# The dummy products that TensorE runs in the waits of the delta-rule core and of the attention and RWKV core are taken out

## The chip, the cores and the metric

The kernel runs on one core of one Trainium2 chip. The metric is device time in microseconds; the median of three runs stands for a kernel. The core has five engines that run at the same time, each through its own list of instructions in order: TensorE (PE: products of matrices; its weight loads are shown apart as PEld), VectorE (DVE), ScalarE (ACT), GpSimd (POOL) and SyncE (SP, which issues the transfers here). Engines wait for one another by semaphores. TensorE's clock has two levels, 1.2 and 2.4 GHz; the profile tells which was granted when, as a share of full speed.

## What is computed

Two transformer blocks on one sequence of 256 tokens, width 1024, float32. The first is two layers of gated feed-forward networks around a mixer: a short convolution in layer 0, a gated delta rule in layer 1. The second block mixes sparse attention (8 heads of 64, in three branches) with an RWKV-7 recurrence (8 heads of 64) and ends in a convolutional feed-forward network.

The two recurrences are computed in chunks of 64 tokens. The delta rule, for 16 value heads with a 128 x 128 state each:

```python
a = jnp.where(strict, jnp.einsum("bhncd,bhnsd->bhncs", k_beta, k) * decay, 0.0)
t_inv = lax.linalg.triangular_solve(eye + a, jnp.broadcast_to(eye, a.shape), left_side=True, lower=True)
...
v_new = u_n - jnp.einsum("bhcd,bhde->bhce", w_n, state)
o = jnp.einsum("bhcd,bhde->bhce", q_g_n, state) + jnp.einsum("bhcs,bhse->bhce", qk_n, v_new)
state = state * jnp.exp(gl_n)[..., None, None] + jnp.einsum("bhcd,bhce->bhde", k_tail_n, v_new)
```

RWKV-7, whose reference is a step per token:

```python
sa = jnp.einsum('bhvk,bhk->bhv', state, a_t)
state = state * w_t[:, :, None, :] + sa[..., None] * b_t[:, :, None, :] + v_t[..., None] * k_t[:, :, None, :]
y = jnp.einsum('bhvk,bhk->bhv', state, r_t)
```

## The kernel before

Most of the time goes into products with weights. SP streams them in tiles of 256 KB, ScalarE and VectorE split each into a high and a low part (L389, L399), and TensorE multiplies high by high, low by high and high by low (L425 to L427). In two stages no weights are streamed, and TensorE works on small products between other engines' steps:

- The delta rule. `GatedDelta.core_pe` runs for four blocks B of four value heads, one behind the other. A block computes keys by keys and keys by queries (L1535, L1536), sums of log decays (L1541, L1546), inverts eight triangular 64 x 64 pairs (`Inverse.pe`), joins the halves (L1484, L1490), and then goes through the chunk: values (L1557), state (L1563), state by keys and queries (L1570, L1571), and outputs (L1576, L1579, L1583). VectorE, ScalarE and GpSimd turn one product's result into the next one's operand.
- The mixer of the second block. `nsa_pe` runs attention for eight units u: scores of unit u + 1 (`scores_pe`, L2200, L2201), then, when VectorE has made the matrix P of unit u, its transposes (L2164, L2166) and the values of unit u - 1 (`values_pe`, L2188). After it the RWKV core's `core_pe` runs for two blocks Bt of four heads: 32 products of decayed keys and queries (L2384 to L2387), the same `Inverse.pe`, two sets of products (L2397, L2405), and four steps c. In each step but the first TensorE multiplies the state M (L2422, L2423), waits for VectorE's N1, multiplies it by the inverse (L2430), waits for SA, and multiplies again (L2438); after every second step come the outputs (L2448, L2449).

`Inverse.pe` transposes, multiplies and waits for five levels: per level two transposes of each half (L950), then 8 products of 64 x 64 by 32 columns (L958), and 16 products (L965) behind VectorE's masked copy. It begins with 16 products in `start_pe` (L944).

TensorE follows its list in order. Between a group of products and the wait that follows it, this list has calls of `keep_clock` (L481), which multiplies the identity by a matrix of ones (128 x 128 each, float32) a given number of times into a PSUM bank that holds nothing of use at that moment; nobody reads the result and no semaphore is tied to it. There are 25 such products in each delta-rule block (4 in the inversion, 5 before it, 7, 3 and 6 after it), 8 in each attention unit, and 35 in each RWKV block (4 in the inversion, 4 before the steps, and three times 3 in each of the steps 1 to 3): 234 in all, each of which is two records of the trace, as all float32 products here are.

Of the kernel before, what the change touches and what calls it, by code (L numbers as in the profile page):

```python
# [19 lines left out]
P = 128  # L20
# [167 lines left out]
def build(nc, ins, out, stages):  # L188
# [28 lines left out]
    with ctx:  # L217
# [262 lines left out]

        def keep_clock(pe, count, bank=aux[1]):  # L481

            for _ in range(count):
                nc.tensor.matmul(bank[:, 0:P], ident[:, :], ones[:, :], start=True, stop=True)  # L484
# [416 lines left out]
        class Inverse:  # L901
# [107 lines left out]
            def pe(self, pe, r):  # L1009

                hs = range(len(self.parts))
                for h in hs:
                    self.start_pe(pe, r, h)
                keep_clock(pe, 4)
                for l in range(1, self.levels):
                    for h in hs:
                        self.x_pe(pe, r, l, h)
                    for h in hs:
                        self.u_pe(pe, r, l, h)
# [16 lines left out]
        class GatedDelta:  # L1036
# [478 lines left out]
            def core_pe(self, pe, B):  # L1515
# [32 lines left out]
                keep_clock(pe, 5)  # L1548
# [10 lines left out]
                keep_clock(pe, 7, acc[0][0])  # L1559
# [6 lines left out]
                keep_clock(pe, 3, acc[0][0])  # L1566
# [6 lines left out]
                keep_clock(pe, 6, acc[0][0])  # L1573
# [113 lines left out]
        class Mixer:  # L1687
# [436 lines left out]
            def nsa_pe(self, pe):  # L2124
# [28 lines left out]
                for u in range(8):  # L2153
# [3 lines left out]
                    keep_clock(pe, 8, acc[0][0])  # L2157
# [213 lines left out]
            def core_pe(self, pe, Bt):  # L2371
# [36 lines left out]
                keep_clock(pe, 4, acc[0][1])  # L2408
                for c in range(4):
# [3 lines left out]
                    if c:  # L2413
                        keep_clock(pe, 3, tr[1])
                        pe.wait_ge(DV.sem, DV.at["M", Bt, c - 1])
                        pe.wait_ge(AC.sem, AC.at["RM", Bt, c - 1]) if c > 1 else None

                        for h in range(4):
                            p, hp = h // 2, h % 2
                            r = slice(64 * hp, 64 * hp + 64)  # L2420
                            bank = (acc[1][1], aux[1])[hp]
                            nc.tensor.matmul(bank[rows, p * ND:(p + 1) * ND], self.al[r, 2 * Bt + p, tt], self.M[r, p, :], start=True, stop=True)  # L2422
                            mm = nc.tensor.matmul(bank[rows, (2 + p) * ND:(3 + p) * ND], self.rt[r, 2 * Bt + p, tt], self.M[r, p, :], start=True, stop=True)  # L2423
                        mm.then_inc(PE.sem, PE.one(("aM", Bt, c)))
                    if c:
                        keep_clock(pe, 3, tr[1])
# [6 lines left out]
                    keep_clock(pe, 3, tr[1]) if c else None  # L2433
# [535 lines left out]
```

## Time and profile before

| | us |
|---|---|
| median of 3 runs | 1920.25 |
| lowest and highest of them | 1908.2, 1920.41 |
| profiled execution | 1930.85 |
| its span, first to last instruction | 1928.9 |
| PE busy | 1794.8 (93%) |
| DVE busy | 1047.9 (54%) |
| ACT busy | 879.0 (46%) |
| POOL busy | 179.6 (9%) |
| PE's share of the chain that ended last | 84% |
| mean granted clock of TensorE | 0.929 |

Busy times are of one profiled execution. The ends of matrix products are modelled, so a busy TensorE need not be one at full rate. The chain that ended last is followed back from the last instruction, at each step to what released it or to the instruction before it on its engine. A timeline's row tells the start and the length in us, the engine, the line of the kernel, the operation, what it writes and reads, and in brackets how long the engine had been idle and who ended that.

### The profile page before, as it was taken

How to read it: one execution, taken by the hardware profiler on the slowest of the kernel's cores; microseconds unless marked ns; L12 is line 12 of the kernel's file. 1: busy time of each engine (PE TensorE's matmuls, PEld its weight loads, DVE VectorE, ACT ScalarE, POOL GpSimd, SP SyncE). 2: the span in 40 equal slices, each digit the busy share in tenths (PEclk: the TensorE clock that was granted, in tenths of full speed). 3: DMA queues.
4: the chain of work that ended last, by engine and by line, in shares of the span. 5: the costliest groups of instructions: out<-in, count | busy, mean ns of one | idle time of the engine just before them, and what ended most of it. 6: DMA issues, size and time to landing. Idle time of an engine off the chain costs nothing.

```text
span 1928.9 us, 27023 instructions
## 1 busy us (share of the span) xinstructions
PE 1794.8 (93%) x10743; PEld 1496.7 (78%) x10743; DVE 1047.9 (54%) x1731; ACT 879.0 (46%) x1381; POOL 179.6 (9%) x184
## 2 busy tenths in 40 slices
PE   6999999999999999788899999989785887999999
PEld 5888888888888888677788888878674776878887
DVE  4555666554755567644465655564234332556664
ACT  5444556543644466422254654454233111546663
POOL 1000010000000011122230000020102001111220
PEclk9999999999999989899899999998596865999999
DMA  7666656555665544300045665574000000645552
GB/s 234 186 185 187 196 181 190 186 186 175 208 186 184 173 158 145 95 2 2 2 140 164 212 187 184 185 204 126 1 1 0 2 2 1 186 154 185 175 183 101
DMA packets 212879, 262.93 MB, mean 136 GB/s; under 512 B 25947, under 2 KB 149266, under 8 KB 212754
## 3 DMA queue, kind: packets, MB, share of 16 engines
q1 hardware_dynamic: 212754, 261.21, 43.5%
q8 instruction: 86, 1.41, 0.3%
q14 instruction: 39, 0.32, 0.1%
HBM read 260.09 MB, written 1.05 MB: 135 GB/s over the span
## 4 chain that ended last, share of the span: by engine, by line
PE 84%; DVE 8%; ACT 2%; POOL 2%; issue 1%; SPq 1%; DMA 0%; DVEq 0%; ACTq 0%; POOLq 0%
PE acc L425 22%; PE acc L427 21%; PE acc L426 21%; DVE low L399 2%; PE acc L484 2%; PE aux L2134 1%; DVE gdn_cv L1282 1%; PE acc L958 1%; PE tr L484 1%; PE tr L669 1%; PE acc L965 1%; POOL gdn_U L1513 1%; PE aux L950 1%; PE tr L950 1%; PE tr L497 1%
## 5 line engine op out<-in xcount | busy, mean ns | idle before, releaser
L399 DVE TENSOR_TENSOR low<-raw,high 128x1024 fp32r<-128x1024 f32 x487 | 592.7, 1238 | 410.9 <-ACT high L389 404.5
L389 ACT ACTIVATE high<-raw 128x1024 fp32r<-128x1024 f32 x487 | 502.3, 1049 | 412.1 <-PE acc L427 387.3
L425 PE MATMUL acc<-high,xh 128*128 128x512 f32 x1360 | 538.5, 396 | 15.5 <-DVE low L399 11.8
L427 PE MATMUL acc<-high,xl 128*128 128x512 f32 x1360 | 529.7, 390 | 0.0
L426 PE MATMUL acc<-low,xh 128*128 128x512 f32 x1360 | 529.3, 389 | 0.0
L425 PEld LDWEIGHTS acc<-high,xh 128*128 128x128 f32 x1360 | 259.3, 191 | 67.4 <-DVE low L399 13.0
L427 PEld LDWEIGHTS acc<-high,xl 128*128 128x128 f32 x1360 | 259.2, 191 | 53.5
L426 PEld LDWEIGHTS acc<-low,xh 128*128 128x128 f32 x1360 | 259.5, 191 | 49.5
L425 PE MATMUL acc<-high,hh 128*128 128x512 f32 x600 | 237.7, 396 | 3.2 <-DVE hl L2059 3.2
L427 PE MATMUL acc<-high,hl 128*128 128x512 f32 x600 | 234.8, 391 | 0.0
L426 PE MATMUL acc<-low,hh 128*128 128x512 f32 x600 | 234.7, 391 | 0.0
L425 PEld LDWEIGHTS acc<-high,hh 128*128 128x128 f32 x600 | 113.4, 189 | 26.0 <-DVE low L399 3.6
L427 PEld LDWEIGHTS acc<-high,hl 128*128 128x128 f32 x600 | 113.3, 189 | 24.1
L426 PEld LDWEIGHTS acc<-low,hh 128*128 128x128 f32 x600 | 113.5, 189 | 22.7
L590 POOL TENSOR_TENSOR rstd<-msq,mhalf 128x1 f32<-128x1 f32 x12 | 6.6, 553 | 776.1 <-DVE msq L572 776.1
L653 ACT ACTIVATE gate_s<-acc,prs 128x256 f32<-128x256 f32 x88 | 41.4, 475 | 44.8 <-PE acc L427 44.8
L659 DVE SCALAR_TENSOR_TENSOR prod<-acc,prs,gate_s 128x256 f32<-128x256 f32 x96 | 45.8, 482 | 19.4 <-ACT gate_s L653 18.1
L506 ACT ACTIVATE xh<-tr,vec 128x128 fp32r<-128x128 f32 x128 | 36.5, 370 | 35.8 <-PE tr L497 35.7
L484 PE MATMUL acc<-ones,ident 128*128 128x128 f32 x272 | 44.4, 326 | 4.0 <-DVE mix_cs L2283 4.0
L484 PEld LDWEIGHTS acc<-ones,ident 128*128 128x128 f32 x272 | 41.9, 237 | 7.8 <-DVE mix_cs L2283 4.7
L515 DVE SCALAR_TENSOR_TENSOR xl<-tr,vec,xh 128x128 fp32r<-128x128 f32 x128 | 35.8, 345 | 22.1 <-ACT xh L506 22.1
L1282 DVE SCALAR_TENSOR_TENSOR gdn_cv<-tr,vec,gdn_cv 128x255 f32<-128x255 f32 (+2 forms) x96 | 38.9, 475 | 13.2 <-ACT gdn_cv L1257 13.2
(431 smaller groups left out, 1768.9 us busy)
## 6 DMA issues: line engine op xcount, KB each, us to landing
raw<-in_ffn_w_gate_up SPq DMA_DIRECT2D x352, 256.0 KB, 3.2
raw<-in_ffn_w_down SPq DMA_DIRECT2D x176, 256.0 KB, 3.0
raw<-in_gdn_w_in SPq DMA_DIRECT2D x96, 256.0 KB, 3.0
raw<-in_ffn_up SPq DMA_DIRECT2D x88, 256.0 KB, 3.1
raw<-in_w_in SPq DMA_DIRECT2D x72, 256.0 KB, 3.0
raw<-in_sc_w_in SPq DMA_DIRECT2D x48, 256.0 KB, 3.1
raw<-in_ffn_down SPq DMA_DIRECT2D x44, 256.0 KB, 2.9
raw<-in_gdn_w_out SPq DMA_DIRECT2D x32, 256.0 KB, 3.0
```

Source lines behind the costliest of these rows:

```text
L389: nc.scalar.activation(high[t % HIGHS][:, 0:n], raw[t % RAWS][:, 0:n], ACT.Copy).then_inc(high_ready, 1)
L399: nc.vector.tensor_tensor(low[t % RAWS][:, 0:n], raw[t % RAWS][:, 0:n], high[t % HIGHS][:, 0:n].bitcast(F32), ALU.subtract).then_inc(low_r ...
L425: nc.tensor.matmul(o, a, wh, start=(k0 + kk == 0), stop=False)
L426: nc.tensor.matmul(o, a, wl, start=False, stop=False)
L427: mm = nc.tensor.matmul(o, b, wh, start=False, stop=(k0 + kk == k - 1))
L484: nc.tensor.matmul(bank[:, 0:P], ident[:, :], ones[:, :], start=True, stop=True)
L506: nc.scalar.activation(xh[:, ch, tb * P:(tb + 1) * P], tr[u % 2][:, i * P:(i + 1) * P], ACT.Copy, scale=s.g0(ch)).then_inc(xh_ready, 1)
L515: x = nc.vector.scalar_tensor_tensor(xl[:, ch, tb * P:(tb + 1) * P], tr[u % 2][:, i * P:(i + 1) * P], s.g0(ch), xh[:, ch, tb * P:(tb + 1) ...
L653: nc.scalar.activation(gate_s[gi % 2][tb][:, :], acc[gi % 2][tb][:, 0:256], ACT.Silu, scale=prs[:, tb:tb + 1]).then_inc(silu_ready, 1)
L659: nc.vector.scalar_tensor_tensor(prod[gi % 2][tb][:, 0:256], acc[gi % 2][tb][:, 256:512], prs[:, tb:tb + 1], gate_s[gi % 2][tb][:, :], ALU ...
L950: mm = nc.tensor.transpose(self.bt[h][:, i * 64:(i + 2) * 64], U[:, p[i]:p[i] + 2, :].rearrange("p j c -> p (j c)"), ident[:, :])
L1282: x = nc.vector.scalar_tensor_tensor(o, tr[u % 2][:, c * SEQ:(c + 1) * SEQ - k], vcol("gdn_conv", (3 - k) * 32 + 2 * s + c), o, ALU.mult, ...
```

## The change

All calls of `keep_clock` are taken out, and the helper with them. Every other instruction and every wait stays, in the same order.

```diff
--- before.py
+++ after.py
@@ -478,11 +478,6 @@
                 pe.wait_ge(tr_free[u % 2], u // 2)
 
 
-        def keep_clock(pe, count, bank=aux[1]):
-
-            for _ in range(count):
-                nc.tensor.matmul(bank[:, 0:P], ident[:, :], ones[:, :], start=True, stop=True)
-
 
 
 
@@ -1011,7 +1006,6 @@
                 hs = range(len(self.parts))
                 for h in hs:
                     self.start_pe(pe, r, h)
-                keep_clock(pe, 4)
                 for l in range(1, self.levels):
                     for h in hs:
                         self.x_pe(pe, r, l, h)
@@ -1545,7 +1539,6 @@
                     for j in range(4):
                         mm = nc.tensor.matmul(bDT[a][:, j * P:(j + 1) * P], self.gm[:, 4 * a + j, :], upto[:, :], start=True, stop=True)
                 mm.then_inc(self.g_D_psum, 1)
-                keep_clock(pe, 5)
                 pe.wait_ge(self.g_A_ready, 8 * B + 8)
                 pe.wait_ge(self.g_DT_ready, 2 * B + 2)
                 self.inv.pe(pe, B)
@@ -1556,21 +1549,18 @@
                 for v in range(4):
                     mm = nc.tensor.matmul(bV[:, v * P:(v + 1) * P], self.U[:, 2 * v, :], self.vb[:, 0, 4 * B + v, :], start=True, stop=True)
                 mm.then_inc(self.g_v0_psum, 1)
-                keep_clock(pe, 7, acc[0][0])
                 pe.wait_ge(self.g_vt_ready, 4 * B + 4)
                 pe.wait_ge(self.g_qk_ready, B + 1)
                 for a in range(2):
                     mm = nc.tensor.matmul(bS[:, a * 256:(a + 1) * 256], self.kt[:, 0, 2 * B + a, :],
                                           self.vt[:, 2 * a:2 * a + 2, :].rearrange("p v e -> p (v e)"), start=True, stop=True)
                 mm.then_inc(self.g_S_psum, 1)
-                keep_clock(pe, 3, acc[0][0])
                 pe.wait_ge(self.g_S_ready, B + 1)
                 for a in range(2):
                     s_ = self.S[:, 2 * a:2 * a + 2, :].rearrange("p v e -> p (v e)")
                     nc.tensor.matmul(bKS[:, a * 256:(a + 1) * 256], self.kf[:, 2 * B + a, P:], s_, start=True, stop=True)
                     mm = nc.tensor.matmul(bQS[:, a * 256:(a + 1) * 256], self.qf[:, 2 * B + a, P:], s_, start=True, stop=True)
                 mm.then_inc(self.g_kS_psum, 1)
-                keep_clock(pe, 6, acc[0][0])
                 pe.wait_ge(self.g_r_ready, 4 * B + 4)
                 for v in range(4):
                     mm = nc.tensor.matmul(bV[:, v * P:(v + 1) * P], self.U[:, 2 * v + 1, :], self.vt[:, v, :], start=True, stop=True)
@@ -2154,7 +2144,6 @@
                     if u < 7:
                         self.scores_pe(pe, u + 1)
                     pe.wait_ge(DV.sem, DV.at["Pc"])
-                    keep_clock(pe, 8, acc[0][0])
                     pe.wait_ge(DV.sem, DV.at["P", u])
                     if u:
                         pe.wait_ge(AC.sem, AC.at["PT", u - 1])
@@ -2405,13 +2394,11 @@
                         mm = nc.tensor.matmul((tr[0], tr[1])[hf][64 * (h % 2):64 * (h % 2) + 64, (tb * 2 + h // 2) * ND:(tb * 2 + h // 2 + 1) * ND],
                                               self.kt[rows, tb, k:k + ND], self.vt[rows, tb, k:k + ND], start=True, stop=True)
                 mm.then_inc(PE.sem, PE.one(("kv", Bt)))
-                keep_clock(pe, 4, acc[0][1])
                 for c in range(4):
                     tb, hf = c // 2, c % 2
                     rows = slice(64 * hf, 64 * hf + 64)
                     tt = slice(64 * c, 64 * c + 64)
                     if c:
-                        keep_clock(pe, 3, tr[1])
                         pe.wait_ge(DV.sem, DV.at["M", Bt, c - 1])
                         pe.wait_ge(AC.sem, AC.at["RM", Bt, c - 1]) if c > 1 else None
 
@@ -2422,15 +2409,12 @@
                             nc.tensor.matmul(bank[rows, p * ND:(p + 1) * ND], self.al[r, 2 * Bt + p, tt], self.M[r, p, :], start=True, stop=True)
                             mm = nc.tensor.matmul(bank[rows, (2 + p) * ND:(3 + p) * ND], self.rt[r, 2 * Bt + p, tt], self.M[r, p, :], start=True, stop=True)
                         mm.then_inc(PE.sem, PE.one(("aM", Bt, c)))
-                    if c:
-                        keep_clock(pe, 3, tr[1])
                     pe.wait_ge(DV.sem, DV.at["N1", Bt, c])
                     for h in range(4):
                         j = (h // 2) * 4 + (h % 2) * 2 + tb
                         mm = nc.tensor.matmul(acc[0][0][rows, h * ND:(h + 1) * ND], self.U[rows, j, :], self.N1[rows, h, :],
                                               start=True, stop=True)
                     mm.then_inc(PE.sem, PE.one(("TN", Bt, c)))
-                    keep_clock(pe, 3, tr[1]) if c else None
                     pe.wait_ge(DV.sem, DV.at["SA", Bt, c])
                     if c < 3:
                         for h in range(4):
```

## Rows read from the trace of the kernel before

**Rows 1.** Page, the span in 40 slices of 48.2 us: TensorE's granted clock in tenths.

```profile
PEclk9999999999999989899899999998596865999999
```

**Rows 2.** The dummy products' line: count, nanoseconds min/median/max, first and last start.

```profile
L484 PE MATMUL acc<-ones,ident x272: 272/275/580, 843.1 to 1590.2; 128*128 128x128 f32 x136
```

**Rows 3.** Windows: length, busy PE, PEld, DVE, ACT, POOL (count), PEclk, DMA share, GB/s.

```profile
814.00:972.60 158.60, 137.44 (x2149) 115.87 (x2148) 67.87 (x284) 38.44 (x93) 40.98 (x46) 0.93 0.01 2
1389.00:1452.00 63.00, 55.28 (x354) 43.46 (x352) 21.17 (x78) 20.28 (x73) 0.00 (x0) 0.91 0.00 1
1499.20:1551.60 52.40, 45.86 (x690) 40.23 (x690) 20.15 (x79) 6.24 (x18) 0.00 (x0) 0.84 0.01 2
1551.60:1621.00 69.40, 64.25 (x689) 55.77 (x690) 20.21 (x78) 6.24 (x18) 0.61 (x1) 0.57 0.01 1
```

**Rows 4.** Timeline (start, length, engine, line, tiles [idle before]): delta rule, tail of block 1.

```profile
877.85 0.68 PE L1490 MATMUL acc<-gdn_X,gdn_T 64*64 64x64 f32 x16 [0.62 <-DVE gdn_X L1501]
880.18 2.05 PE L1557 MATMUL aux<-gdn_vb,gdn_U 128*128 128x128 f32 x8 [1.65 <-DVE gdn_U L1505]
882.02 3.19 PE L484 MATMUL acc<-ones,ident 128*128 128x128 f32 x14
...
882.90 1.03 DVE L1634 TENSOR_SCALAR gdn_vt<-gdn_vn,gdn_etail 128x128 f32<-128x128 f32 x4 [1.67 <-ACT gdn_vn L1599]
...
885.01 1.26 PE L1563 MATMUL tr<-gdn_vt,gdn_kt 128*128 128x256 f32 x4
...
886.96 0.70 PE L1570 MATMUL acc<-gdn_S,gdn_kf 128*128 128x256 f32 x2
...
888.79 1.50 PE L484 MATMUL acc<-ones,ident 128*128 128x128 f32 x12
```

**Rows 5.** Timeline of TensorE, same block's successor: start of the inversion, high clock.

```profile
900.85 0.68 PE L944 MATMUL aux<-ident,gdn_A 64*64 64x64 f32 x16
...
901.93 1.16 PE L484 MATMUL aux<-ones,ident 128*128 128x128 f32 x8
903.42 0.44 PE L950 MATMUL aux<-ident,gdn_Uc 128*128 128x128 f32 x2 [0.33 <-DVE gdn_Uc L1007]
...
905.80 0.44 PE L950 MATMUL aux<-ident,gdn_Uc 128*128 128x128 f32 x2
```

**Rows 6.** Timeline of TensorE, RWKV block 1: the same inversion level, low clock.

```profile
1569.16 0.69 PE L950 MATMUL aux<-ident,rw_U 128*128 128x128 f32 x2
...
1572.69 0.69 PE L950 MATMUL aux<-ident,rw_U 128*128 128x128 f32 x2
```

**Rows 7.** Timeline, attention: scores (L2200), dummies (L484), transposes (L2164) at either clock.

```profile
1400.57 0.79 PE L2200 MATMUL acc<-mix_kf,mix_qf 64*128 64x128 f32 x2
...
1403.43 3.78 PE L484 MATMUL acc<-ones,ident 128*128 128x128 f32 x16
...
1410.65 0.48 PE L2200 MATMUL acc<-mix_kf,mix_qf 64*128 64x128 f32 x2
...
1412.16 2.05 PE L484 MATMUL acc<-ones,ident 128*128 128x128 f32 x16
...
1420.55 2.05 PE L484 MATMUL acc<-ones,ident 128*128 128x128 f32 x16
1424.09 0.55 PE L2164 MATMUL acc<-ident,mix_S 128*128 128x128 f32 x3 [1.50 <-DVE mix_S L2298]
...
1441.14 1.01 DVE L2298 TENSOR_SCALAR mix_S<-mix_S,mix_coef 128x128 f32<-128x128 f32 x4
...
1444.22 2.05 PE L484 MATMUL acc<-ones,ident 128*128 128x128 f32 x16
```

**Rows 8.** Timeline, RWKV block 1: dummies, the vector add waited for, next products.

```profile
1606.39 1.65 PE L484 MATMUL tr<-ones,ident 128*128 128x128 f32 x6
...
1606.70 0.27 DVE L2570 TENSOR_TENSOR rw_N<-aux,rw_gv 64x128 f32<-64x128 f32 x1
...
1607.97 1.11 PE L2430 MATMUL acc<-rw_N,rw_U 64*64 64x64 f32 x8
```

## The prediction

> **What bounds the kernel now.** I read the page's slices of the granted clock first [rows 1]. TensorE is busy nearly throughout, and its clock is nearly full except for dips in slices 15 to 20 and a long low in slices 28 to 34. The gated-delta rule lies in slices 17 to 21, the attention and the RWKV-7 recurrence in the long low. Every dummy product stands in these two stretches, from 820 to 1618 us [rows 2], none in the matrix products that stream weights. So I cut the kernel by stage [rows 3]: the delta rule (158.6 us, mean clock 0.93), the eight attention units (63.0, 0.91), and the two RWKV blocks, which run the same program (52.4 at 0.84, and 69.4 at 0.57). No weights stream there (DMA share 0.01), and none is waited for. TensorE and VectorE (or ScalarE) take turns in one chain, so each step's time is TensorE's part, which depends on its clock, plus the other engine's part, which doesn't.
>
> The two RWKV blocks show what the clock is worth: same instructions, 17.0 us apart. They also show that dummies don't hold the clock everywhere: the second block has as many as the first, and ran at the low level almost whole. There the inversion's small products (64 rows by 32 columns) with dummies between the steps after it did not bring the clock back.
>
> **What the change removes.** 234 products, each two records of the trace (the line's 272 records on acc among them [rows 2]). At the high clock 16 records take 2.05 us, at the low one 3.78 [rows 7], so a record costs 0.108 us more at the low level. No wait, no semaphore and no other instruction changes. The direct effect can only be a gain, where a group of dummies ends after the thing that the products behind it wait for. The indirect effect is on the clock, and can only be a loss here.
>
> *Direct gains.* At the high clock almost nothing: behind dummies TensorE still waits 0.33 us in the inversion's start [rows 5] and 1.50 us in an attention unit [rows 7]. The exception is the last attention unit: its matrix was ready at 1442.15 (1441.14 + 1.01), and the dummies start at 1444.22 [rows 7], so their 1.9 us are pure delay. At the low clock dummies are in the way: in the second RWKV block the vector add ends at 1606.97 and the products that need it start at 1607.97, behind dummies that began at 1606.39 [rows 8]. 1.0 us; the block has eleven such places (one in the inversion's start, one before the first step, nine in the three later steps). I take 0.9 each, 10 us. In the delta rule's tail the dummies push L1563 from 883.93 (882.90 + 1.03) to 885.01 [rows 4], 1.1 us, which I count in two blocks of four.
>
> *The clock.* First, where it would fall. In the tail of a delta-rule block TensorE has two groups of sixteen records of half-height products with idle times of 0.62 and 1.65 us around them [rows 4], and the clock falls there: the next 14 dummy records take 2.99 us (882.02 to 885.01), 0.214 each, and 12 records later at 888.79 only 1.50. In between the clock rose, over the dense stretch of products and dummies. Without dummies the start of the inversion becomes as sparse as that tail: L944's 32 half-height records in 1.08 us (900.85 to 901.93), then 1.49 us of nothing until 903.42 [rows 5], and before L944 the wait that another dummy group fills now. I therefore expect the clock to fall there too, and then to stay low through the inversion, since the same inversion in the second RWKV block never brought it up. It can rise only where full-height products stand close together, from L1570 of one block to L1546 of the next.
>
> *The delta rule.* One inversion level takes 2.38 us at the high level (903.42 to 905.80 [rows 5]) and 3.53 at the low one (1569.16 to 1572.69 [rows 6]): 1.15 more, five levels, 5.75. L944 doubles its 1.08 at most, and L1484 with L1490 are as many records of the same kind: 0.9 each, so 7.5 in all. In the tail L1570 and L1571 (1.83 us from 886.96 to 888.79 [rows 4]) and the 24 records of L1576, L1579 and L1583 (24 x 0.108 = 2.6) would add 4.4 if the clock stayed low all the way; I take half, 2.2. A block that falls costs 9.7. I take three blocks of four, since block 0 starts its inversion behind a longer dense stretch: 29, plus 1 for block 0's tail, less 2.2 for the delays: +28. If the last tail stays low, the first weight products behind it run at half speed until the clock rises: +2. Bounds: no block falls, +3 (tails alone); all four fall with whole tails, 4 x 11.9 = +48.
>
> *Attention.* Of 63.0 us at mean clock 0.91, 18% or 11 us were low and 52 high. Of these 52, five waits of 3.54 us (1420.55 to 1424.09 [rows 7]) and the last dummies' 1.9 are not real products; that leaves 32 us of them. At the low level the scores take 2.86 us (1400.57 to 1403.43) against 1.51 (1410.65 to 1412.16) [rows 7], a factor of 1.9. The clock rises over dummies here: the 16 records at 1403.43 take 3.78 us, those at 1412.16 take 2.05 [rows 7]. A unit lasts 8.39 us (1412.16 to 1420.55); less the 3.54 that leaves 4.85 us of mostly half-height products and, without dummies, 3.54 of nothing, sparser than the second RWKV block that stayed low. So all is low: 32 x 0.86 = 27.5, less the 1.9: +25. Bounds: +5, if the clock rises and holds in most units; +28.
>
> *RWKV.* The first block becomes what the second is now without its delays: 69.4 - 10 = 59.4 against 52.4, +7. The second loses its 10 but starts with the 64 records of L2384 to L2387 low instead of high, 64 x 0.108 = 6.9: -3. Bounds for both together: -14 (no new low stretch) and +8.
>
> Sum: 28 + 2 + 25 + 7 - 3 = +59. The profiled execution took 1930.85 us (span 1928.9), which gives 1990. The three runs shown lie at 1920.25 in the middle and 1908.2 at the lowest, 10.6 and 22.7 below it; the sum on the median is 1979. Part of this spread may be the clock of the second RWKV block (17.0 us are at stake there), a chance that goes away when everything is low, so the new runs may lie nearer to the profile's sum. I forecast **1984**.
>
> **A rule against the rows.** A level that grows from 2.38 to 3.53 us loses a third of its low time, not half [rows 5, 6], as VectorE's part doesn't stretch. The Trainium skill ("TensorE: Matmul & The Clock Gate", section "Terms") puts the penalty of throttling at the throttled time times (1 - K/N), which is half at the half clock. By that rule some 240 us of newly low time here (an estimate: 118 in the delta rule, 77 in attention, 49 in RWKV) would cost about 120 less the gains of 14, and give 2037; by the rows it is 59. The same page says (Part 1, "What's actually happening") that the throttled state is the default and activity releases it, which speaks against this change as the rows do.
>
> **Rivals.**
> - *The clock holds in the delta rule.* The real products there are dense enough that the inversion starts at the high level in most blocks. For it: inversions at full clock keep it with idle time in every level, and the gap is short. Against it: the tails, alike in density, fall every time. Then +3 to +8 instead of +30: 1958. Chance 0.17.
> - *Faster: dummies only delay.* If the clock's pattern did not depend on the dummies, what remains is 10 in the second RWKV block, 4 in the first one's low part (four or five such places), 2.2 in the delta rule and 1.9 in attention: -18, 1912 on the profile and 1902 on the median. The second block, low in spite of dummies, speaks for it; the rise in attention under the first 16 dummy records against. It decides if the high stretches lose less than 18 us. Chance 0.05.
> - *No difference.* The clock recovers in attention and the first RWKV block by real products, and its remaining losses of 10 to 20 are paid by the delays removed: 1925. Chance 0.07.
> - *Waits stretch too.* Every newly low stretch costs half of its length: 2037. No row shows a VectorE time that depends on TensorE's clock. Chance 0.03.
> - *Forecast*: low from the inversions on, in attention and RWKV whole: 1984, its own range 1965 to 2003. Chance 0.68.
>
> **Range and chances.** About 1% is what a measurement of this kernel can tell from no change. 8 in 10 reach from the second-best case's lower part to the forecast with all four delta blocks low: 1945 to 2006. Slower by over 1% (above 1939.5) hold the forecast, the first rival and the last: 0.88. Within 1%: 0.08. Faster: 0.04.
>
> **What would show it.** Right: spacing of inversion levels 3.5 us in delta blocks 1 to 3, one attention unit about 12.7 us (4.85 x 1.9 + 3.54) from L2164 to L2164 against 8.4, both RWKV blocks near 59 to 66, clock 0.5 in all of 1336 to the end of RWKV but for a few microseconds at its dense transposes; VectorE's single instructions unchanged. Wrong: levels at 2.4 in the delta rule (first rival), or attention units under 9 us. I would be wrong above all if the real products alone lift the clock where I read that only dummies did.

## The result and the profile after

| us | before | after |
|---|---|---|
| median | 1920.33 (4 runs) | 1984.66 (4 runs) |
| single runs | 1908.20, 1920.25, 1920.41, 1926.98 | 1976.89, 1977.77, 1991.55, 1991.75 |
| profiled execution | 1930.85 | 1976.89 |
| its span | 1928.9 | 1974.8 |
| mean granted clock of TensorE | 0.929 | 0.885 |

The change makes the kernel slower: the ratio of after to before is 1.034, with a 95% interval of 1.027 to 1.042. On the medians that is 64 us. Taking TensorE's unread products out costs 3.4% of the time.

First the page of the kernel after, its granted clock in tenths over 40 slices of 49.4 us:

```profile
PEclk9999999999999989666689999998556656999999
```

Against [rows 1] slices 17 to 20, the delta rule, have fallen from 8 and 9 to 6, and in the second block's mixer slice 30, in attention, has fallen from 9 to 5 and slice 32 from 8 to 6. No other slice differs by more than one tenth.

Then the windows of the stages after: length, busy PE, PEld, DVE, ACT, POOL (with counts), granted clock, DMA share, GB/s. The rows are the delta rule, attention from its first products (those with compressed keys, L2139) to the last values (L2177), and the two RWKV blocks.

```profile
813.30:1005.80 192.50, 153.98 (x1952) 117.45 (x1952) 69.98 (x283) 38.80 (x92) 41.85 (x47) 0.64 0.01 1
1404.00:1504.40 100.40, 70.77 (x288) 51.17 (x288) 28.95 (x104) 24.18 (x89) 2.99 (x1) 0.56 0.00 0
1550.70:1610.20 59.50, 47.84 (x620) 40.42 (x620) 20.61 (x79) 6.22 (x18) 0.00 (x0) 0.56 0.01 2
1610.20:1667.90 57.70, 45.53 (x620) 39.67 (x620) 19.71 (x78) 6.22 (x18) 0.61 (x1) 0.62 0.01 2
```

[Rows 3] has the same stages of before, with ends read a little differently (158.60 and 69.40 us), and attention only from unit 0's transposes (1389) on. For the table below these are the windows of before: the delta rule, attention from its first products on, as in the second row above, and RWKV block 1.

```profile
813.50:972.30 158.80, 137.94 (x2152) 116.37 (x2150) 67.61 (x284) 38.43 (x92) 41.48 (x46) 0.92 0.01 2
1369.30:1451.70 82.40, 69.80 (x416) 56.23 (x416) 28.96 (x104) 24.21 (x89) 2.99 (x1) 0.81 0.00 1
1551.60:1621.40 69.80, 64.65 (x690) 56.04 (x690) 20.21 (x78) 6.24 (x18) 0.61 (x1) 0.57 0.01 1
```

| stage, us | before | after | difference |
|---|---|---|---|
| delta rule | 158.8 | 192.5 | +33.7 |
| attention | 82.4 | 100.4 | +18.0 |
| RWKV block 0 | 52.4 | 59.5 | +7.1 |
| RWKV block 1 | 69.8 | 57.7 | -12.1 |
| everything else | 1565.5 | 1564.7 | -0.8 |
| span | 1928.9 | 1974.8 | +45.9 |

Nearly all of the difference is in the stages that lost dummies. In the delta rule VectorE, ScalarE and GpSimd were busy for nearly as long as before (69.98, 38.80 and 41.85 us against 67.61, 38.43 and 41.48), TensorE for 16 us longer though it issued 200 records fewer.

Now one level of the delta rule more closely: the timeline of TensorE after, in block 0, where the first column is the start and the second the length in us.

```profile
819.16 1.95 PE L1540 MATMUL acc<-upto,gdn_gm 128*128 128x128 f32 x16
822.37 0.68 PE L939 MATMUL aux<-ident,gdn_A 64*64 64x64 f32 x16 [1.27 <-ACT gdn_qk L1585]
822.86 0.66 PE L939 MATMUL tr<-ident,gdn_A 64*64 64x64 f32 x16
824.93 0.69 PE L945 MATMUL aux<-ident,gdn_Uc 128*128 128x128 f32 x2 [1.41 <-DVE gdn_Uc L1002]
...
828.47 0.69 PE L945 MATMUL aux<-ident,gdn_Uc 128*128 128x128 f32 x2
```

Before, the same place of block 0 reads:

```profile
820.70 1.28 PE L484 MATMUL aux<-ones,ident 128*128 128x128 f32 x10
822.12 0.68 PE L944 MATMUL aux<-ident,gdn_A 64*64 64x64 f32 x16
822.61 0.66 PE L944 MATMUL tr<-ident,gdn_A 64*64 64x64 f32 x16
823.20 1.16 PE L484 MATMUL aux<-ones,ident 128*128 128x128 f32 x8
824.69 0.44 PE L950 MATMUL aux<-ident,gdn_Uc 128*128 128x128 f32 x2 [0.33 <-DVE gdn_Uc L1007]
```

The dummies are now idle time of 1.27 and 1.41 us; the inversion starts at nearly the same time (824.93 and 824.69, in stages that begin at 813.3 and 813.0), but its first transposes take 0.69 us instead of 0.44, and the level lasts 3.54 us (824.93 to 828.47) instead of 2.38 [rows 5]. The granted clock fell at 824.2 and rose at 858.4 again. That VectorE's part does not change is seen in its masked copy, whose numbers are nanoseconds min, median and max, in before and after:

```profile
L981 DVE TENSOR_TENSOR gdn_X<-acc,lvmask x80: 214/220/226, 825.6 to 953.5; 128x64 f32<-128x64 f32 x80
```

```profile
L976 DVE TENSOR_TENSOR gdn_X<-acc,lvmask x80: 212/220/226, 826.3 to 985.1; 128x64 f32<-128x64 f32 x80
```

In attention the timeline of after shows three units one behind the other, and the one in which the clock rose:

```profile
1444.31 0.87 PE L2153 MATMUL acc<-ident,mix_S 128*128 128x128 f32 x3 [3.53 <-DVE mix_S L2287]
...
1456.81 0.87 PE L2153 MATMUL acc<-ident,mix_S 128*128 128x128 f32 x3 [3.52 <-DVE mix_S L2287]
...
1469.30 0.87 PE L2153 MATMUL acc<-ident,mix_S 128*128 128x128 f32 x3 [3.52 <-DVE mix_S L2287]
...
1473.18 1.09 PE L2177 MATMUL aux<-mix_PT,mix_vt 128*64 128x128 f32 x8
...
1479.30 0.61 PE L2153 MATMUL acc<-ident,mix_S 128*128 128x128 f32 x3 [3.52 <-DVE mix_S L2287]
```

A unit lasts 12.50 us (1444.31 to 1456.81) against 8.39 before. The wait for VectorE is 3.52 or 3.53 us in each, at either level of the clock. From 1472.8 to 1479.6 the clock was high, from within one unit's values on, and that spacing is 10.00 us (1469.30 to 1479.30).

### The profile page after: what moved, and what is told of

It reads as the page before. It is cut to its first block, busy times and chain, and to the rows that moved or that the text cites. A ratio compares the mean times of both kernels' runs of the same rounds, so it can differ in the third digit from the quotient of the medians.

```text
span 1974.8 us, 26088 instructions
## 1 busy us (share of the span) xinstructions
PE 1792.0 (91%) x10275; PEld 1474.1 (75%) x10275; DVE 1050.5 (53%) x1731; ACT 878.8 (44%) x1381; POOL 179.5 (9%) x184
## 4 chain that ended last, share of the span: by engine, by line
PE 83%; DVE 10%; ACT 2%; POOL 1%; issue 1%; SPq 1%; DMA 0%; DVEq 0%; ACTq 0%
PE acc L425 21%; PE acc L427 21%; PE acc L426 21%; PE acc L953 2%; DVE low L399 2%; PE aux L2124 1%; DVE gdn_cv L1276 1%; PE tr L664 1%; PE aux L945 1%; PE tr L945 1%; PE acc L960 1%; PE tr L2177 1%; PE aux L2177 1%; PE tr L492 1%; PE acc L2190 1%
## 5 line engine op out<-in xcount | busy, mean ns | idle before, releaser
L425 PEld LDWEIGHTS acc<-high,xh 128*128 128x128 f32 x1360 | 259.3, 191 | 67.4 <-DVE low L399 13.1
L426 PEld LDWEIGHTS acc<-low,hh 128*128 128x128 f32 x600 | 113.2, 189 | 22.5
L1276 DVE SCALAR_TENSOR_TENSOR gdn_cv<-tr,vec,gdn_cv 128x255 f32<-128x255 f32 (+2 forms) x96 | 38.8, 473 | 13.3 <-ACT gdn_cv L1251 13.3
L2702 DVE SCALAR_TENSOR_TENSOR ffn_conv<-tr,vec,ffn_conv 128x255 f32<-128x255 f32 (+1 forms) x88 | 35.3, 474 | 6.7 <-ACT ffn_conv L2687 6.6
L2200 ACT ACTIVATE mix_S<-mix_S,mix_nm 128x128 f32<-128x128 f32 (+1 forms) x32 | 14.1, 443 | 53.6 <-DVE mix_nm L2241 53.6
```

The lines of the kernel that those rows point to most:

```text
L425: nc.tensor.matmul(o, a, wh, start=(k0 + kk == 0), stop=False)
L426: nc.tensor.matmul(o, a, wl, start=False, stop=False)
L1276: x = nc.vector.scalar_tensor_tensor(o, tr[u % 2][:, c * SEQ:(c + 1) * SEQ - k], vcol("gdn_conv", (3 - k) * 32 + 2 * s + c), o, ALU.mult, ...
```

## The experiments

Times are medians with their range, ratios are to the kernel before, timed beside the experiment on the same chip, with a 95% interval. The experiments ran in three series, and the kernel before had medians of 1927.49, 1910.64 and 1926.03 in them (13, 13 and 19 runs), so small differences between series mean nothing. Its 45 single runs lie apart: 13 from 1903.5 to 1910.6, 4 near 1919 and 1920, and 28 from 1924.6 to 1933.9.

### Which stage has the loss: dummies taken out of one stage at a time

**RWKV's 70 dummies out, all others kept** (`self.tag` tells which of the two cores an inversion belongs to).

```diff
-                keep_clock(pe, 4)
+                if self.tag == "gdn_inv":
+                    keep_clock(pe, 4)
...
-                keep_clock(pe, 4, acc[0][1])
...
-                        keep_clock(pe, 3, tr[1])
...
-                    if c:
-                        keep_clock(pe, 3, tr[1])
...
-                    keep_clock(pe, 3, tr[1]) if c else None
```

> Only the 70 dummy products of the two RWKV blocks are out; delta rule and attention keep theirs. My theory (each stage's clock hangs on its own dummies): delta rule 159 us and attention 82 us as before, first RWKV block 59.5 us (before 52.4, it ran 59.5 in the changed kernel), second 58 to 66 us (before 69.8, changed 57.7): 1917 to 1924 us in all, the same as before within 0.3%. Rival (the RWKV dummies are worth their time): both blocks over 60 us, 1930 or more. Rival (a stage's clock depends on what ran long before it): attention or delta rule change by over 3 us.

Measured: 1930.88 us (1923.9 to 1934.0), ratio 1.004 [1.001, 1.007]. The windows of its two RWKV blocks:

```profile
1501.30:1560.40 59.10, 47.47 (x620) 40.00 (x620) 20.63 (x79) 6.23 (x18) 0.00 (x0) 0.59 0.01 2
1560.40:1625.00 64.60, 53.42 (x620) 45.87 (x620) 20.19 (x78) 6.23 (x18) 0.62 (x1) 0.50 0.01 1
```

The first block loses 6.7 us, the second wins 5.2, both as expected; the total is over the expected 1917 to 1924, beside a kernel before of 1927.49. RWKV's dummies are worth almost nothing by the medians: in the profiled executions they hold the clock in the first block and only delay in the second. That is not so in every execution: 13 of the 45 runs of the kernel before took under 1911 us, and none of the ten here took under 1923.9; and further down half-width dummies in the same places left the second block at 52.8 us, clock 0.84.

**Only the delta rule's dummies kept** (the edit above, and in attention):

```diff
-                    keep_clock(pe, 8, acc[0][0])
```

> Dummies only in the delta rule (100 products), none in attention and RWKV. My theory: delta rule 159 us, attention 100 us as in the changed kernel, RWKV as there: before + 18 - 5, 1933 us. If attention's dummies were worth nothing it would be 1915; if the loss in attention were carried by the delta rule's low clock, attention would be at 82 to 90 us here.

Measured: 1950.07 us (1949.15 to 1951.4), ratio 1.014 [1.007, 1.021]. Against the kernel above that is 19.2 us for the attention dummies alone. Its windows of attention and of RWKV block 1:

```profile
1370.30:1476.90 106.60, 76.97 (x288) 55.51 (x288) 28.93 (x104) 24.21 (x89) 3.00 (x1) 0.50 0.00 1
...
1584.30:1641.90 57.60, 45.48 (x620) 39.67 (x620) 19.71 (x78) 6.23 (x18) 0.62 (x1) 0.62 0.01 2
```

Attention is low from end to end here, 24.2 us longer than before; in the kernel after 11 us of the stage were high (1472.8 to 1479.6, and from 1500.1 to its end). RWKV block 1 took 57.6 us, though its program is that of the kernel above, where it took 64.6: in one execution the clock rose within its inversion, in the other it did not. These 7.0 us are in the 19.2 though they are RWKV's, whose instructions are the same in both; by the stage itself attention's dummies are worth 24.2. The expectation, 1933, was 17 us too low: attention was put at 100 us, from the one profile in which its clock had risen, and the kernel before stood 7 us higher in this series (1927.49 against 1920.33).

**Only attention's dummies kept.**

```diff
-                keep_clock(pe, 4)
...
-                keep_clock(pe, 5)
...
-                keep_clock(pe, 7, acc[0][0])
...
-                keep_clock(pe, 3, acc[0][0])
...
-                keep_clock(pe, 6, acc[0][0])
```

(and RWKV's, as above)

> Dummies only in the eight attention units (64 products), none in the delta rule and RWKV. My theory: delta rule 192 us, attention 82 us, RWKV as in the changed kernel: before + 34 - 5, 1949 us. Together with the run that keeps only the delta rule's, the two losses must add up to the whole change (18 + 34 - 5 = 47) if the stages don't depend on one another.

Measured: 1967.92 us (1959.21 to 1968.77), ratio 1.021 [1.013, 1.030]. The delta rule took 194.9 us, its four blocks 52.4, 47.3, 48.1 and 47.2, as in the kernel after (50.4, 47.0, 48.2, 46.9). By the medians its dummies are worth 37.0 us (1967.92 less 1930.88). The expected 1949 was missed by 19 us, 7 of them again the kernel before, and 7 RWKV block 1, which took 64.6 us here. The three parts, 3.4 + 19.2 + 37.0, put together on this series' 1927.49 give 1987; the change itself measured 1984.66, so the stages' losses add up to within 3 us.

### Which of the delta rule's dummies do it

**Only the nine at the start of an inversion kept** (five before it, four in it; everything else out):

```diff
-                keep_clock(pe, 7, acc[0][0])
...
-                keep_clock(pe, 3, acc[0][0])
...
-                keep_clock(pe, 6, acc[0][0])
```

> As the changed kernel, but the delta rule keeps the 9 dummy products at the inversion's start in each block (5 before it, 4 in it), not the 16 behind it. My theory (the clock falls in the inversion's start and then can't rise): these 9 hold it through the inversions, levels at 2.38 us; the tail from L1557 on runs low until the next dense stretch, so the delta rule takes 165 to 172 us (159 before, 192 changed); in all 1953 to 1965. Rival (the tail's dummies decide, since they lift the clock again before the next inversion): delta rule near 190.

**Only the sixteen of the tail kept:**

```diff
-                keep_clock(pe, 4)
...
-                keep_clock(pe, 5)
```

> As the changed kernel, but the delta rule keeps the 16 dummy products behind the inversion (7, 3, 6), not the 9 at its start. My theory: the clock rises over them as before and falls at the next inversion's start: levels at 3.5 us in most blocks, delta rule 181 to 188 us; 1968 to 1982 in all. Rival: delta rule near 160 to 168, if a clock that is high well before the inversion stays high through it.

Measured: 1965.15 us (1958.28 to 1969.63), ratio 1.023 [1.015, 1.031], and 1974.21 us (1966.93 to 1982.26), ratio 1.028 [1.020, 1.036]. The windows of the delta rule, with the start's dummies kept, and with the tail's:

```profile
813.00:984.90 171.90, 137.80 (x2024) 109.01 (x2024) 67.55 (x283) 38.64 (x92) 42.14 (x47) 0.81 0.01 2
```

```profile
813.60:993.90 180.30, 157.50 (x2080) 128.62 (x2080) 69.85 (x283) 38.86 (x92) 42.00 (x47) 0.71 0.01 2
```

158.8 us have become 171.9 without the tail's dummies (+13.1) and 180.3 without the start's (+21.5); the sum is 34.6, and both out gave 33.7. With the start's dummies kept block 0 ran its whole inversion high and was low from 840.8 to 851.1, in its tail; with the tail's kept it was low from 824.5 to 851.9, where with neither it was low to 858.4. So the start's dummies hold the clock through the inversion. The tail's lift it again sooner: without them the low stretches in the tail last 10 to 20 us instead of 3 to 7 before.

### Is it TensorE being busy that matters, or with what

**All dummies at half height:** 64 rows instead of 128, same number, same columns.

```diff
-                nc.tensor.matmul(bank[:, 0:P], ident[:, :], ones[:, :], start=True, stop=True)
+                nc.tensor.matmul(bank[:, 0:P], ident[0:64, :], ones[0:64, :], start=True, stop=True)
```

> All 234 dummies stay where they are, but each uses only 64 of the 128 rows of the array (identity and ones cut to 64 partitions), the same 128 columns and the same time each. Theory A (the clock follows how much of the array works, so rows count): the clock falls as in the changed kernel, attention about 100 us or more, and the dummies' delays stay: 1985 to 2000 us. Theory B (only TensorE's busy time counts): the clock as before, 1920 us.

**All dummies at half width:** all 128 rows, but weights of 64 columns, so that as much of the array takes part as at half height.

```diff
-                nc.tensor.matmul(bank[:, 0:P], ident[:, :], ones[:, :], start=True, stop=True)
+                nc.tensor.matmul(bank[0:64, 0:P], ident[:, 0:64], ones[:, :], start=True, stop=True)
```

> All 234 dummies stay, but each uses all 128 rows and only 64 of the 128 columns of the array (the identity cut to 64 columns, ones whole); the moving operand has 128 columns as before. The half-height run took 2001 us, with attention at 108.7. Theory A1 (rows fed with data are what counts): the clock as in the kernel before, attention 82 us, 1920 us. Theory A2 (the area of the array at work counts): as the half-height run, attention near 107, 1985 to 2003 us.

Measured: half height 2000.92 us (1998.27 to 2004.56), ratio 1.040 [1.033, 1.047]; half width 1918.12 us (1914.26 to 1933.98), ratio 0.999 [0.996, 1.003]. Half height is worse than no dummies at all (1984.66 and 1983.67 in two measurements), half width is as good as whole ones. Windows of attention, at half height and at half width:

```profile
1391.60:1500.30 108.70, 98.67 (x416) 79.49 (x416) 28.98 (x105) 24.21 (x89) 2.99 (x1) 0.51 0.00 1
```

```profile
1373.50:1457.00 83.50, 70.39 (x416) 55.61 (x416) 28.97 (x105) 24.21 (x89) 3.00 (x1) 0.79 0.00 1
```

The same 416 records in both. With half-height dummies TensorE was busy for 98.67 of 108.70 us, 91%, and its clock stood at 0.51; with half-width ones it was busy for 84% at 0.79. The records themselves cost the same at the high clock (the line of the dummies, half height and half width, ns min, median, max):

```profile
L484 PE MATMUL aux<-ones,ident x88: 272/272/577, 821.8 to 1635.3; 64*128 64x128 f32 x88
```

```profile
L484 PE MATMUL aux<-ones,ident x88: 272/273/473, 821.4 to 1569.0; 128*64 128x128 f32 x88
```

So neither the time that dummies take in TensorE's list nor the share of the array that they fill (the same half in both kernels) explains what they do for the clock. The height is what is left: whole and half-height dummies differ in nothing else. Which 64 rows are used, and whether the values in them matter, no run tests. Half-height ones are not quite without effect: in the delta rule (180.9 us, between 158.8 and 192.5) the clock still held through the inversions, and then was low for 17 us from each tail on. In attention and in both RWKV blocks (70.6 and 76.0 us) they brought nothing and took their time at the low level. It also fits that the real products of 64 rows, which are most of those in an inversion and in RWKV, leave TensorE busy and its clock low: in block 0 of the kernel after it was busy for 28.32 of the 34.20 us from 824.2 to 858.4, at 0.50. But height is not all: of the 32 records of an attention unit only the 8 of the scores are of 64 rows and 20 are of 128 rows, and without dummies, with TensorE idle for 3.5 of 12.5 us, its clock was low too.

### Can more be had: dummies where TensorE still waits, none where it doesn't

**RWKV refitted.** Eleven dummies in the long wait before the inversion, which had none; fewer in the steps, where they ended after the thing waited for.

```diff
                 pe.wait_ge(AC.sem, AC.at["A", Bt, 1])
+                keep_clock(pe, 11, acc[0][0])
                 pe.wait_ge(DV.sem, DV.at["RB", Bt, 1])
...
-                        keep_clock(pe, 3, tr[1])
+                        if c != 2:
+                            keep_clock(pe, 3, tr[1])
...
-                        keep_clock(pe, 3, tr[1])
+                        keep_clock(pe, 2, tr[1])
...
-                    keep_clock(pe, 3, tr[1]) if c else None
+                    keep_clock(pe, 2, tr[1]) if c else None
```

> Only the RWKV part of the run before this one: 11 dummy products in the wait for the masks in each block, and the three trims in the steps. Theory: the inversion starts at the high clock in both blocks (levels 2.38 us), 46 to 48 us per block: 1896 to 1905. If the clock falls in the inversion's start in spite of them, 59 to 70 for the second block and 1920.

Measured: 1905.72 us (1899.34 to 1911.73), ratio 0.994 [0.990, 0.998]. Its RWKV blocks:

```profile
1500.10:1547.90 47.80, 43.73 (x695) 38.20 (x695) 20.06 (x79) 6.23 (x18) 0.02 (x1) 0.93 0.01 2
1547.90:1595.20 47.30, 43.70 (x694) 38.19 (x694) 19.63 (x78) 6.23 (x18) 0.59 (x1) 0.93 0.01 2
```

Both run at 0.93 now, where the second had been at 0.57 [rows 3]. Which of the two edits does it, the eleven added dummies or the fewer ones in the steps, no run separates. The median gained only 5 us on this series' 1910.64, less than the 27 us of the profiles: the kernel before itself probably has executions in which RWKV does better than in its profile; none of them was profiled.

**All stages refitted.** As above, and in the delta rule two dummies before the join's second products and seven before L1557; in attention none in the last unit, where they were pure delay [rows 7].

```diff
                 mm.then_inc(self.g_last_x, 1)
+                keep_clock(pe, 2, acc[1][0])
...
                 self.last_pe(pe, B)
+                keep_clock(pe, 7, acc[1][0])
...
-                    keep_clock(pe, 8, acc[0][0])
+                    if u < 7:
+                        keep_clock(pe, 8, acc[0][0])
```

> The kernel before with dummies in three waits that had none: 2 and 7 products around the join of the halves in the delta rule (L1490, L1557), 11 in the wait for the masks in each RWKV block; and without those that only delay: the last attention unit's 8, RWKV's 3 behind the outputs, and 2 instead of 3 in two places of a step. Theory: the clock no longer falls in these waits; delta rule 159 to about 152 us, RWKV blocks 52.4 and 69.8 to 46 to 48 each, attention 82 to 80: 1890 to 1900 us, faster by 1 to 2%. If the clock falls there all the same, the added products only delay: 1920 or more.

> The fill-all kernel once more, beside the one with more dummies in attention: 1884 to 1896 us again, 1 to 2% below the kernel before.

Measured: 1887.45 us (1883.75 to 1896.32), ratio 0.983 [0.976, 0.991], and the same kernel in another series 1900.1 us (1886.94 to 1918.27), ratio 0.988 [0.983, 0.992]; the first is a little under the expected 1890 to 1900, the second over the expected 1884 to 1896. Windows of the first of the two: delta rule, attention, RWKV blocks 0 and 1.

```profile
813.30:966.40 153.10, 140.70 (x2221) 117.89 (x2222) 67.08 (x284) 38.42 (x92) 42.84 (x48) 0.98 0.01 2
1365.90:1445.90 80.00, 67.42 (x400) 53.95 (x400) 28.95 (x104) 24.21 (x89) 2.99 (x1) 0.81 0.00 1
1491.50:1536.40 44.90, 40.73 (x695) 35.34 (x695) 20.05 (x79) 6.23 (x18) 0.02 (x1) 1.00 0.01 2
1536.40:1580.80 44.40, 40.71 (x694) 35.32 (x694) 19.64 (x78) 6.24 (x18) 0.60 (x1) 1.00 0.01 2
```

This is the best version found, faster than both kernels: 1.2 to 1.7% below the one before, 4 to 5% below the one after (1887.45 and 1900.1 against 1984.66). But for its first microseconds the whole delta rule ran at the high level, with blocks of 40.7, 37.8, 37.8 and 36.9 us against 41.1, 39.9, 38.8 and 39.0 before, and so did both RWKV blocks. In the second profile one of the delta rule's tails and parts of both RWKV blocks were low again (155.2, 47.8 and 51.8 us), so the placement is not yet safe against chance.

**The same with 14 dummies instead of 8 in seven attention units.**

```diff
-                        keep_clock(pe, 8, acc[0][0])
+                        keep_clock(pe, 14, acc[0][0])
```

> The fill-all kernel (1887 us) with 14 instead of 8 dummies in each attention unit but the last, 3.0 us of the 3.5 us wait at the high clock. In the fill-all run one unit of six fell and took 11.2 us instead of 8.4. Theory: no unit falls any more, but at the low clock with which the first units start 14 dummies take 6.2 us, 2.7 more than the wait: attention 78 to 82 us against 80.0, 1884 to 1890. Rival: the longer groups lift the clock no earlier and only delay while it is low: attention 83 or more.

Measured: 1900.42 us (1895.23 to 1911.82), ratio 0.989 [0.981, 0.997], the same as the 1900.1 us of the refitted kernel in the same series, and above the expected 1884 to 1890. Its windows of attention's units and of RWKV block 0:

```profile
1394.90:1452.00 57.10, 56.09 (x410) 45.24 (x408) 21.17 (x78) 20.12 (x73) 0.00 (x0) 1.00 0.01 1
...
1497.20:1551.80 54.60, 50.71 (x695) 44.14 (x695) 20.07 (x79) 6.23 (x18) 0.04 (x1) 0.78 0.01 2
```

All units ran high now, where with 8 dummies one of them still fell (11.21 or 11.25 us instead of 8.39), but the whole stage took 78.8 us against 80.0. RWKV, with the same program as in the refitted kernel, had 54.6 and 54.1 us in this profile, where the others had 44 to 52. So what attention can still give is small beside what chance moves in RWKV.

### The change once more

> The change as it is, once more, on the chip of the other runs of this call: 1975 to 1992 us in two clusters, as in its first runs, 3 to 4% above the kernel before. If attention is at low clock throughout it takes 106.6 us, and the whole about 1981 to 1991.

Measured: 1983.67 us (1976.5 to 1990.05), ratio 1.033 [1.025, 1.040]; delta rule 192.5, attention 100.5, RWKV 59.5 and 57.7. It repeats the change's profile to 0.1 us in every stage.

## Why the prediction was right, and where not

The sign, the size and the main mechanism were right: 1984 us were forecast, within 1945 to 2006, and 1984.66 was measured, with a repeat at 1983.67. That the two numbers agree within a microsecond is luck: the term of the delta rule was too small and those of attention, RWKV block 1 and the weight products too large, and the profiled executions lie at different ends of their spreads (1930.85 is near the top of the kernel before's, 1976.89 the lowest of after's). On profiled times the sum said 1990 and 1976.89 came.

| term, us | forecast | profiled | by medians, one stage's dummies out at a time |
|---|---|---|---|
| delta rule | +28 (3 to 48) | +33.7 | +37.0 |
| attention | +25 (5 to 28) | +18.0, +24.2 where low throughout | +19.2, with 7.0 of RWKV's in it |
| RWKV block 0 | +7 | +7.1 | |
| RWKV block 1 | -3 | -12.1, or -5.2 | +3.4 for both blocks |
| first weight products | +2 | -0.8 for all else | |

*The step on block 0* failed. "I take three blocks of four, since block 0 starts its inversion behind a longer dense stretch" had nothing behind it but the look of the timeline. Block 0 fell like the others, at 824.2, in this profile, in the repeat (50.41 us against 50.40), in the kernel with only attention's dummies (52.39) and in the one with only the tail's (low from 824.5). The one block in which the clock held a little longer was block 1, where it fell at 875.4, behind a first level of 2.38 us; in blocks 2 and 3 it fell at 919.8 and 967.6, at the inversion's start. In the repeat it was block 2 that held longer. A block lost 9.3, 7.1, 9.4 and 7.9 us, a mean of 8.4, against 9.7 less 0.55 for the delays. So the count was too low and the price too high.

*The split within the delta rule* was off more than its sum. The start was put at 7.5 us in three blocks, 22.5, and measured 21.5 over four. The tail was put at 2.2 each and one more in block 0, less the delays, 5.4 in all, and measured 13.1. "I take half" was the guess; the low stretches there last 10 to 20 us without dummies, nearly as long as the whole tail.

*The level's price* was right: 1.15 us forecast, 1.16 measured (3.54 less 2.38). The rival in which the clock holds in the delta rule fell with it.

*Attention.* A unit was put at "about 12.7 us" and took 12.50 us in three of its seven spacings and in five where the clock never rose (12.48 to 12.50); the wait of 3.54 us stayed at 3.52. "Mostly half-height products" was a misreading: 8 of a unit's 32 records are of 64 rows. The price didn't use it, but the argument that a unit is sparser than an RWKV block did. Where it ran low throughout, the term was 24.2 against the 25 forecast. What failed is "So all is low": in the change's own profile and its repeat the clock rose for 6.8 us behind a unit's values, which saves 2.5 us in that unit, and again behind the last one; 6.2 us in the stage. In three profiled kernels with the same attention program the stage took 106.6, 106.6 and 102.7 us.

*RWKV.* Block 0 came as worked out (59.5 against 59.4). The delay of the dummies in block 1 [rows 8] was read rightly; the timeline of after, the same vector add and the same product:

```profile
1657.38 0.27 DVE L2554 TENSOR_TENSOR rw_N<-aux,rw_gv 64x128 f32<-64x128 f32 x1
1657.71 1.11 PE L2415 MATMUL acc<-rw_N,rw_U 64*64 64x64 f32 x8 [0.57 <-DVE rw_N L2554]
```

The product starts 0.06 us after the add's end (1657.38 + 0.27) instead of 1.00. But "the same inversion in the second RWKV block never brought it up" was taken for a rule and is none. In the profile of after the clock rose in that very inversion; the timeline of its levels:

```profile
1628.08 0.69 PE L945 MATMUL aux<-ident,rw_U 128*128 128x128 f32 x2
...
1631.15 0.44 PE L945 MATMUL aux<-ident,rw_U 128*128 128x128 f32 x2
...
1633.53 0.44 PE L945 MATMUL aux<-ident,rw_U 128*128 128x128 f32 x2
```

The levels behind 1631.15 take 2.38 us, until the clock falls again at 1643.4. That is worth 6.9 us (64.6 against 57.7), and no instruction of RWKV decides it: kernels with the same RWKV program had 64.6 in three profiles and 57.6 or 57.7 in four.

*"A chance that goes away when everything is low"* was wrong for this reason. The four runs of after lie in two pairs, 1977 and 1992, 14 us apart, and the mean granted clock of the pairs is 0.885 and 0.877. Block 1 (6.9) and attention (6.2) together would give 13.1 of these 14; that they do is likely but not shown, as no execution of the upper pair was profiled.

*Rule against rows.* The estimate by the Trainium skill ("TensorE: Matmul & The Clock Gate", section "Terms"), that half of the throttled time is lost, gave 2037; the measurement sides with the rows. A part of that gap is the 240 us of newly low time, which was put too high: the mean clocks, 0.929 over 1928.9 us and 0.885 over 1974.8, give 180. Half of these, less the 14 of gains, would be 76 us, and 45.9 came.

The rows of one level say why half is too much, and VectorE's part, which the prediction gave as the reason, is the smaller one. TensorE idled 4.9 us before L965 for VectorE's copies in the delta rule of before, 0.24 in each level, and 0.2 us in that of after. This is the group of L965 in the two windows, before and after (records, busy us, mean ns of one, idle us before them and what ended it):

```profile
L965 PE MATMUL acc<-gdn_X,gdn_T 64*64 64x32 f32 x640 | 17.0, 222 | 4.9 <-DVE gdn_X L981 4.9
```

```profile
L960 PE MATMUL acc<-gdn_X,gdn_T 64*64 64x32 f32 x640 | 25.3, 290 | 1.2 <-DVE gdn_X L976 0.2
```

Without this wait a level is 2.14 us at the high and 3.54 at the low level of the clock, a factor of 1.65: TensorE's own small products don't take twice as long. The timeline of after, 16 of them at the low and 16 at the high level:

```profile
825.55 0.66 PE L953 MATMUL acc<-gdn_Uc,gdn_A 64*64 64x32 f32 x16
826.14 0.69 PE L945 MATMUL tr<-ident,gdn_Uc 128*128 128x128 f32 x2
...
873.45 0.43 PE L953 MATMUL acc<-gdn_Uc,gdn_A 64*64 64x32 f32 x16
873.82 0.44 PE L945 MATMUL tr<-ident,gdn_Uc 128*128 128x128 f32 x2
```

From their start to the next product are 0.59 and 0.37 us, a factor of 1.6. In an attention unit VectorE's part is the larger reason: TensorE's part grows from 4.85 to 8.98 us, by 1.85, and the wait of 3.52 us keeps the loss at a third.

*The rival "waits stretch too"* had no support: the masked copy's median is the same. One VectorE group did take longer: the four operations of L1624 (L1634 before), which took 1.03 us [rows 4] and, in the timeline of block 0's tail after:

```profile
849.74 1.18 POOL L1650 TENSOR_SCALAR gdn_gm<-beyond,gdn_g 128x128 f32<-128x128 f32 x2
850.07 0.60 ACT L1589 ACTIVATE gdn_vn<-aux 128x512 f32<-128x512 f32 x1 [5.38 <-PE aux L1550]
850.70 1.45 DVE L1624 TENSOR_SCALAR gdn_vt<-gdn_vn,gdn_etail 128x128 f32<-128x128 f32 x4 [1.67 <-ACT gdn_vn L1589]
```

The longest of the four takes 862 to 936 ns in blocks 0 to 2, where it took 419 to 423 before; in block 3, where GpSimd is all but idle, it takes 287 against 286. So it seems to stretch beside GpSimd's work, not with TensorE's clock (which was low in block 3 too), and some 0.4 us in three tails belong to it; how the two meet was not followed. "VectorE's instructions unchanged" was wrong by that much.

*The rival "dummies only delay"* holds in the profiles for the second block of RWKV alone, where 5.2 us came back with the clock low in most of it either way; the other delays that it lists are far smaller than what the clock cost.

## What to carry to other kernels

Where TensorE takes turns with another engine in small products, read its granted clock by stage before touching anything that seems to be idle work; here products nobody reads are worth 64 us of 1985. Price the loss by one step at either level in the same trace, not by half of the stretch, and give the count of stretches that will fall a wider range than the price of one, since the same instructions came out at either level in different executions. Dummies paid here where they fill a wait ahead of or between small products and end before the thing waited for; where they end later they delay as well.

## What the runs showed of the hardware that was not expected

- Half-height dummies did not do for the clock what whole ones do, at the same number, columns and time of one. With them: 2000.92 us, attention at 0.51 with TensorE busy for 91% of it. Half-width dummies with the same share of the array: 1918.12 us. No dummies: 1984.66.
- Half the clock does not double a level of small products: 16 products of 64 rows by 32 columns took 0.59 us instead of 0.37, and a whole level without its wait 3.54 instead of 2.14.
- The same instructions can run at either clock in the same place. RWKV block 1 without dummies took 57.6 to 64.6 us in seven profiles, attention without them 100.4 to 106.6 in five, and the kernel before spread from 1903.5 to 1933.9 us over 45 runs.
- Eleven dummies in one wait, with fewer in the steps behind it, took RWKV block 1 from a mean clock of 0.57 to 0.93 and from 69.8 to 47.3 us (44.4 to 54.1 in the other profiles with them). The 35 of before had not held it in the profiled execution, though half-width ones in their places did (0.84).
